# Attention stage: three orders of work changed in the first slots

## The reference, cut to what matters

```python
q = _rope(_rms(heads(q, AT_HEADS), qn), pos)          # 8 query heads of 128
k = _rope(_rms(heads(k, AT_KV_HEADS), kn), pos)       # 2 key/value heads
yC = attend(q, k, v, qi, wi, ki).reshape(B, T, AT_W) * jax.nn.silu(g_c)
# attend, after the indexer has chosen 256 keys for each query:
s = jnp.einsum('bqngd,bqknd->bqngk', qg, kg) * Dh ** -0.5
p = jax.nn.softmax(jnp.where(valid, s, -jnp.inf), axis=-1)
out = jnp.einsum('bqngk,bqknd->bqngd', p, vg)
# then
y = jnp.concatenate([yC, yX], axis=-1) @ w_out;  return x + y
```

## Time and profile before

| | us |
|---|---|
| median of three runs | 1876.54 |
| lowest, highest | 1876.25, 1878.46 |
| profiled execution, its time | 1876.28 |
| profiled execution, its span | 1874.7 |

### The profile page before, as it was taken

One profiled execution on the slowest core, in us unless ns is written; L12 is line 12 of the kernel. 1 busy time (PEld: TensorE's weight loads), 2 busy tenths in 40 slices (PEclk: granted clock), 3 DMA queues, 4 the chain that ended last, 5 costly groups with the idle time before them and its releaser, 6 DMA issues. The chain is left out here.

```text
span 1874.7 us, 26519 instructions
## 1 busy us (share of the span) xinstructions
PE 1780.7 (95%) x9417; PEld 1376.2 (73%) x9417; DVE 978.3 (52%) x2277; ACT 601.6 (32%) x1275; POOL 414.0 (22%) x646
## 2 busy tenths in 40 slices
PE   6999999999999997999899999999999689999999
PEld 5666888777788876887776566887777467777887
DVE  5412643233377665211542467888879665675111
ACT  3110332111022112200321346877745445553010
POOL 4301222000133352100342001221005365330000
PEclk9999999999899999999999999999999889999999
DMA  6434333444355467321322111334433874332331
GB/s 212 127 116 121 117 118 108 148 153 133 118 162 185 149 182 262 150 95 52 113 68 77 46 59 67 99 113 138 142 128 102 262 223 133 118 104 84 108 118 45
DMA packets 134349, 236.97 MB, mean 126 GB/s; under 512 B 28486, under 2 KB 60774, under 8 KB 134218
## 3 DMA queue, kind: packets, MB, share of 16 engines
q1 hardware_dynamic: 110506, 171.96, 28.4%
q0 software_dynamic: 17328, 56.24, 9.5%
q10 hardware_dynamic: 6384, 7.08, 1.1%
HBM read 169.05 MB, written 66.17 MB: 125 GB/s over the span
## 5 line engine op out<-in xcount | busy, mean ns | idle before, releaser
L1212 PE MATMUL layer_acc<-layer_w_hi,layer_xT_hi 128*128 128x512 f32 x640 | 262.2, 410 | 0.2 <-PE all_banks L1360 0.2
L1214 PE MATMUL layer_acc<-layer_w_hi,layer_xT_lo 128*128 128x512 f32 x640 | 253.4, 396 | 0.0
L1213 PE MATMUL layer_acc<-layer_w_lo,layer_xT_hi 128*128 128x512 f32 x640 | 252.9, 395 | 0.0
L2773 PE MATMUL front_acc<-front_w_hi,front_xT_hi 128*128 128x512 f32 x520 | 218.8, 421 | 10.4 <-DVE front_w_lo L3314 4.9
L2774 PE MATMUL front_acc<-front_w_lo,front_xT_hi 128*128 128x512 f32 x520 | 206.9, 398 | 0.0
L2775 PE MATMUL front_acc<-front_w_hi,front_xT_lo 128*128 128x512 f32 x520 | 206.9, 398 | 0.0
L1212 PEld LDWEIGHTS layer_acc<-layer_w_hi,layer_xT_hi 128*128 128x128 f32 x640 | 122.0, 191 | 30.6 <-issue 5.9
L1213 PEld LDWEIGHTS layer_acc<-layer_w_lo,layer_xT_hi 128*128 128x128 f32 x640 | 121.4, 190 | 26.7 <-issue 2.6
L1214 PEld LDWEIGHTS layer_acc<-layer_w_hi,layer_xT_lo 128*128 128x128 f32 x640 | 121.0, 189 | 27.0
L2773 PEld LDWEIGHTS front_acc<-front_w_hi,front_xT_hi 128*128 128x128 f32 x520 | 98.9, 190 | 43.9 <-issue 12.2
L3099 ACT ACTIVATE front_index_rows<-odd_bias,front_candidate 128x1024 bf16<-128x1024 f32 (+3 forms) x128 | 124.9, 982 | 8.6 <-DVEq L3463 5.0
(11 more groups left out here) (675 smaller groups left out, 3594.5 us busy)
## 6 DMA issues: line engine op xcount, KB each, us to landing
all_w<-in_w_even POOLq DMA_DIRECT2D x80, 256.0 KB, 3.6
h_even<-layer_st SPq DMA_DIRECT2D x79, 256.0 KB, 2.2
all_w<-in_w_odd POOLq DMA_DIRECT2D x61, 256.0 KB, 3.6
h_odd<-front_st SPq DMA_DIRECT2D x55, 256.0 KB, 2.0
layer_scratch<-h_even SPq DMA_DIRECT2D x46, 256.0 KB, 3.1
all_scratch<-in_w_mem SPq DMA_DIRECT2D x32, 256.0 KB, 3.9
all_scratch<-h_even SPq DMA_DIRECT2D x32, 256.0 KB, 3.5
all_scratch<-x SPq DMA_DIRECT2D x14, 512.0 KB, 3.6
```

The lines of the kernel that those rows point to most:

```text
L1212: T.matmul(out[0:rows, :], xh[:, kk, to], wh[:, r, :], start=(kk == 0), stop=False)
L1213: T.matmul(out[0:rows, :], xh[:, kk, to], wl[:, r, :], start=False, stop=False)
L1214: ins = T.matmul(out[0:rows, :], xl[:, kk, to], wh[:, r, :], start=False, stop=(kk == KC - 1))
L2773: T.matmul(out[0:rows, :], xh[:, k, to], wh[:, r, :], start=(k == 0), stop=False, skip_group_check=True)
```

## The change

Three edits. (1) VectorE follows a plan with `job` ahead of `prep` in every slot, not only in the first ones. (2) GpSimd follows a plan with `prep` ahead of `smp` in slots 0 to 5; later slots are as before. (3) ScalarE requests its 16 value pages in slots 6 to 21, not 0 to 15. With (1), the second row step of p=2 on VectorE is cut in two: the product stays in slot 3, the gains move to slot 4, the rotation to slot 5; TURN of p=2 becomes 5, so its transposes move to slots 6, 7, 8, and SP's store and its next row load by one slot too.

```diff
-def back_plan():
+def back_plan(early=(), job_first=False):
     plan = [[] for _ in range(77)]
+    for s in early:
+        plan[s].append("prep")
     for s in range(1, 40):
         plan[s].append("smp")
+    if job_first:
+        for g in range(67):
+            plan[g].append("job")
     for s in range(57):
-        plan[s].append("prep")
-    for g in range(67):
-        plan[g].append("job")
+        if s not in early:
+            plan[s].append("prep")
+    if not job_first:
+        for g in range(67):
+            plan[g].append("job")
...
-    TURN = {p: 4 if p == 2 else 6 for p in START}
+    TURN = {p: 5 if p == 2 else 6 for p in START}
...
         @block.gpsimd
-            follow(plan, 0, None, prep=preps(), smp=smps(), job=idle(), ...)
+            follow(back_plan(early=range(6)), 0, None, prep=preps(), smp=smps(), job=idle(), ...)
...
         @block.scalar, jobs()
-                    if g < 2 * PAGES:
-                        b, p = divmod(g, PAGES)
+                    if 6 <= g < 6 + 2 * PAGES:
+                        b, p = divmod(g - 6, PAGES)
                         act.dma_start(vp[b][:, p, :], value_page(act, b, p)).then_inc(va_in[b], 16)
...
         @block.vector, preps()
                         if step == 2:
                             dve.wait_ge(rsd, 1)
                             link(V.tensor_tensor(y, y, bc(ssq[u][0:rows, :], 2, HD), ALU.mult))
+                        if step == 3:
                             for lo, hi, j, n in ((0, QH * HD, 0, QH), (QH * HD, QK, 1, KVH)):
                                 part = heads(qk[u][0:rows, lo:hi], n)
                                 link(V.tensor_tensor(part, part, bc(gam[0:rows, j, :], 1, n), ALU.mult))
-                        if step == 3:
+                        if step == 4:
                             rotate(V, link, y, HD // 8, rt[:, PREP[p]], tmp, rows, H10)
                             dve.sem_inc(rq2, 1)
...
-            follow(plan, 0, None, prep=preps(), smp=smps(), job=jobs(), ties=late_ties(), ...)
+            follow(back_plan(job_first=True), 0, None, prep=preps(), smp=smps(), job=jobs(), ties=late_ties(), ...)
```

More of the change, by code:

```diff
@@ L4051, in load_slice @@
                 pool.dma_start(raw[w % RAW], a["w_out_odd"][:, k, 512 * half:512 * half + 512]).then_inc(w_in[w % RAW], 16)
-            follow(plan, 0, None, prep=preps(), smp=smps(), job=idle(), ties=idle(), weights=weights(), out=idle())
+            follow(back_plan(early=range(6)), 0, None, prep=preps(), smp=smps(), job=idle(), ties=idle(), weights=weights(), out=idle())
         @block.tensor
@@ L4545, in outputs @@
                     yield
-            follow(plan, 0, None, prep=preps(), smp=smps(), job=jobs(), ties=late_ties(), weights=weights(), out=outputs())
+            follow(back_plan(job_first=True), 0, None, prep=preps(), smp=smps(), job=jobs(), ties=late_ties(), weights=weights(), out=outputs())
 OUTS = [(1, SEQ, D), (NB, NT, D), (1, 1, NH, HD, HD), (1, 1, NH, HD), (1, 1, NH), (1, NB, NH, HD, HD),
```

## The result

| kernel | median us (lowest to highest, runs) | span of the profiled execution, us |
|---|---|---|
| before, beside it | 1876.29 (1875.40 to 1878.46, 5) | 1874.7 |
| changed | 1887.87 (1883.16 to 1888.46, 5) | 1886.3 |

The account below looks back on a forecast made before the run. TensorE, busy 95%, could gain only where it waits in the last stage, with slot 5's key page the binding link. +0.15 + 1.4 - 0.95 = +0.6 on 1876.28 gave 1876.9 us, no change; range 1872.0 to 1880.8.

Parts of the forecast that it names:

- The two stalls in slots 4 and 5: mix(1) waits 5.54 us for VectorE, turned(4) 1.16 for a key page; without the first, TensorE waits for the same page.
- Part one: Slot 5's key page lands 1.3 us sooner as ScalarE's value pages compete later; bounds 0 to 3.6.
- The low clock: Rival: idle time added in slots 20 and 23 keeps the clock low 10 us more, +5.9, 1882.8 us; chance 0.12.
- Part two: VectorE and GpSimd: p=2's later rotation delays scores(6) by 1.6; slot 12 moves +1.45 less 1.3, +0.15 us.
- The power of p=3: GpSimd's power starts 1.45 us later behind VectorE's later sums, and TensorE waits in slot 12; bounds 0.5 to 2.0.
- p=4: Sums about 1.8 us later; the slip of its slot 20 transposes is hidden by mix(17)'s 2.70 idle.
- Part three: ScalarE's six new requests in slots 16 to 21: two exposed at 0.68 each, +1.4 us; bounds 0 to 4.1.
- The one of slot 21: ScalarE's request there is exposed, about 0.68 us, as ScalarE is full up to the copy TensorE idles for.
- the one of slot 18: ScalarE's request there is exposed, about 0.68 us, ahead of the samples' exponentials, with mix(17) behind them.
- Part four: Job ahead of prep later on: -0.95 us; GpSimd starts 1 to 2 later, covered by transposes three slots further; bounds -0.95 to 0.
- The gain of 0.95: In slots 31 and 39 sums no longer delay y_of, so mix's idles of 0.45 and 0.50 us go.
- The rival of collisions: Different VectorE instructions meet GpSimd's multiplication by the gains, p=5 to 8: -3.2 or +3.2, 1873.7 or 1880.1 us; chance 0.12.

Follow-up runs that it names:

- e7: Kernel before, with SP requesting unit 4's key pages ahead of its row load, bias loads and value stores: 1875.62 us, ratio 1.0000.
- e11: Changed kernel, VectorE's job ahead of prep in slots 0 to 5 only, SP's key pages of unit 4 sooner: 1873.07 us, 0.9981 of before.
- e9: Changed kernel once more without any edit, for a second trace: 1884.86 us, 1.0044 of before.
- e8: Kernel before, with VectorE's job ahead of prep in slot 39 only: 1879.29 us, ratio 1.0017.
- e6: Changed kernel, with GpSimd's first weight requests ahead of prep in slot 39: 1879.78 us, 1.0021 of before.

## Why the prediction was wrong, point by point

- **The two stalls in slots 4 and 5: right.** mix(1)'s stall went and the page's took its place. e7 and e11 show that they lie side by side.
- **Part one, the page, +1.3 sooner: mis-sized.** It came 0.7 sooner (0.2 in e9), and the 1.2 us that the samples' scores took longer at the low clock ate that. The low clock was a rival, but placed at slots 20 to 23; there, from `scores(17)` to `scores(21)`, the changed kernel had more clock than before (0.84 against 0.69). It cost time in slot 5 and behind the 4.53.
- **Part two, the rotation in slot 6: the wait was right** (1.6 forecast, waits of 1.41 and 1.66), what comes back of it wasn't: 0.75 was to be made up behind it, and the shift fell only from 2.00 to 1.83. **The power of p=3: the order's share was right, the sum not.** The forecast's 1.45 holds 0.75 for a late slot 7 (given as 0.85 a few lines ahead of that) and so 0.7 for the order; measured, the order is 0.72. But slot 7 stood at +1.83 and not at 0.75 less 1.3. Slot 12 stands at +2.45 and +1.53 instead of +0.15. p=4 was hidden, as forecast.
- **Part three, ScalarE's requests: small**, as said. The one of slot 21 costs 0.5 (forecast 0.68), and PE's wait in slot 23 went from 1.04 to 1.34. What the one of slot 18 costs isn't shown: it falls into slots 17 to 21, where traces of one kernel differ by 1.7.
- **Part four, the step that failed: "GpSimd's work then starts 1 to 2 us later; the transposes are three slots further, which covers it. Bounds -0.95 to 0."** The gain of 0.95 is half there: -0.49 at slot 32 stays, but of the -0.73 at slot 40, 0.53 comes back at slot 41, where mix now idles 0.29. The rest was wrong twice. The delay is 2.2 to 3.3 us for p=5 to 8, not 1 to 2: after `y_of`, VectorE's `masked` must wait for that slot's scores before the sums run. At slot 28 the cover was 1.5 us, a number the trace of before gives and that I never took from it. And in slot 39 the transposes aren't what is late: it is the weight requests and the multiplication **queued behind** GpSimd's power and product. The forecast doesn't mention them. Their cost, 4.6 us of the 9.8, is shown by e8 (the order of that one slot brings it) and by e6 (with the requests ahead of the power, 0.55 is left).
- **The rival of collisions** had the right rows and was right at p=6, where the multiplication now meets the one-column instruction: +0.8 at slot 35. At p=7 it had the wrong question. Which instruction is met changed little there (the cast pays 1.42, the one-column one paid 1.69). What counts is **when the hold ends**: `y_of` comes after it in both kernels, so a GpSimd chain 2.75 late is a TensorE 2.65 late. Transposes three slots away are no cover for that.
- **The range** (1872.0 to 1880.8) took its ends from parts one to three and held -0.95 to 0 for part four. The delay of part four, priced without cover at slots 28 and 40 (2 x 2), would have put its upper end 4 us higher, at 1884.8; that is still under the 1887.87 measured.

Open: why the low clock lasts longer in one execution than in the next, up to slot 21 and behind the 4.53 us, and with that how much of the +2 to +3 of the early slots the median carries. No edit parted the late slice and the late hold: by the times alone, with the slice there VectorE could have cast and split between 1624.59 and 1626.1, ahead of the multiplication; with no hold `y_of` would be 1.24 late.

## What to carry to other kernels

When an order is changed in every slot for the sake of a few, each producer that moves back needs its own slack, read from the trace: start of the consumer less its wait, less the end of the producer's chain. A producer's delay also hits whatever is queued behind the engine that waits for it, requests for transfers above all, and these belong to other streams. Here the reorder in slots 0 to 5 alone, with the page's request moved up as well, takes 0.9981 of the time of before, where the full change takes 1.0056.

## What the runs showed of the hardware

- After 4.53 us of idle time at the full clock TensorE ran the next matmuls at the low level (2.48 to 2.90 us instead of 1.57; 1.49 instead of 0.82); after 1.58 and 2.13 us in the same place it did not (1.57, 1.58). The one idle time doesn't decide it: in slot 11 of the changed kernel, behind waits of 0.96 and 1.58 us (1505.76, 1507.96), four matmuls took 0.93 us and two score matmuls 1.06, instead of 0.61 and 0.60. The tail of one stall cost 1.7 us in one trace and 3.0 in another.
- A one-column VectorE instruction with two SBUF inputs, or a cast of 512 columns, that starts beside GpSimd's 128x1024 multiplication ends 0.01 to 0.3 us after it: one column took 1.91 and 2.37 instead of 0.22, the cast 1.83 and 1.86 instead of 0.41. The price is what is left of the 2.35 us. A subtraction of 512 columns with two SBUF inputs (L113, before) that started 0.30 us ahead of the multiplication (1645.43 and 1645.73) was held too: 3.21 us instead of 0.69.
- A stage behind an unchanged front starts up to 9 us sooner or later from one execution to the next (1458.5 to 1467.4), so shifts are to be counted from the start of the stage.
